# Block 1 retention: rotary partners by GpSimd multiplications in place of TensorE permutation products

## What is computed

```python
def rotary(x, pos):
    half = HEAD_DIM // 2                     # 32
    inv = 1.0 / (ROPE_BASE ** jnp.linspace(0.0, 1.0, half, dtype=jnp.float32))
    ang = pos[:, None] * inv[None, :]
    cos = jnp.cos(ang)[None, :, None, :]
    sin = jnp.sin(ang)[None, :, None, :]
    x1, x2 = x[..., :half], x[..., half:]
    return jnp.concatenate([x1 * cos - x2 * sin, x2 * cos + x1 * sin], axis=-1)

q = rotary(q.reshape(b, s, RET_HEADS, HEAD_DIM), pos)
k = rotary(k.reshape(b, s, RET_HEADS, HEAD_DIM), pos) * (HEAD_DIM ** -0.5)
```

## Time and profile before

| what | value |
|---|---|
| median of three executions | 3490.95 us |
| the profiled execution | 3486.4 us |
| its span, first to last instruction | 3484.6 us |
| mean granted TensorE clock | 0.988 |
| TensorE busy | 3376.5 us, 97% |
| VectorE busy | 1652.7 us, 47% |
| ScalarE busy | 1226.2 us, 35% |
| GpSimd busy | 199.2 us, 6% |

### The profile page before, as it was taken

The page is one execution under the profiler, slowest core; times in us unless marked ns, Lnnn a source line. Parts: engine busy times, 40 slices in busy tenths (PEclk is TensorE's granted clock), DMA queues, the critical chain, the costliest instruction groups (busy, mean ns, idle before and its releaser), DMA issues.

```text
span 3484.6 us, 42143 instructions
## 1 busy us (share of the span) xinstructions
PE 3376.5 (97%) x15726; PEld 2641.3 (76%) x15726; DVE 1652.7 (47%) x2158; ACT 1226.2 (35%) x1831; POOL 199.2 (6%) x247
## 2 busy tenths in 40 slices
PE   8989999999899999999998999999999999999998
PEld 6657888775688877888775688887888776678887
DVE  6755443566444335443545554434443543654433
ACT  4343122432422234222444442234222444542233
POOL 1200000011010000000002310000000001310000
PEclk9999999999999999999999999999999999999999
DMA  6213322221243222332320143333332321033331
GB/s 167 66 43 84 97 97 96 85 79 49 61 106 99 95 92 79 96 98 96 78 64 24 30 104 96 96 97 87 96 97 100 85 73 32 16 89 96 96 96 67
DMA packets 434262, 288.19 MB, mean 83 GB/s; under 512 B 44528, under 2 KB 412316, under 8 KB 433896
## 3 DMA queue, kind: packets, MB, share of 16 engines
q1 hardware_dynamic: 431272, 280.02, 27.7%
q0 software_dynamic: 2736, 4.58, 0.9%
q10 hardware_dynamic: 144, 2.10, 0.2%
HBM read 284.53 MB, written 2.13 MB: 82 GB/s over the span
## 4 chain that ended last, share of the span: by engine, by line
PE 92%; DVE 3%; ACT 3%; issue 2%; DMA 0%; SPq 0%; DVEq 0%; ACTq 0%
PE bank L1964 27%; PE bank L1966 27%; PE bank L1965 27%; PE bank L1974 2%; PE bank L2061 1%; PE bank L2107 1%; PE bank L2083 1%; PE bank L2184 1%; PE bank L2151 1%; PE bank L2448 1%; PE bank L2450 1%; PE bank L2013 1%; PE bank L2035 0%; ACT whi L927 0%; DVE G L1506 0%
## 5 line engine op out<-in xcount | busy, mean ns | idle before, releaser
L1964 PE MATMUL bank<-hh,whi 128*128 128x512 f32 x2832 | 1140.6, 403 | 36.7 <-DVE hl L1418 22.8
L1966 PE MATMUL bank<-hh,wlo 128*128 128x512 f32 x2832 | 1107.9, 391 | 0.0
L1965 PE MATMUL bank<-hl,whi 128*128 128x512 f32 x2832 | 1107.5, 391 | 0.0
L1368 DVE TENSOR_TENSOR wlo<-raw,whi 128x1024 fp32r<-128x1024 f32 (+2 forms) x534 | 642.5, 1205 | 300.6 <-ACT whi L927 285.8
L1964 PEld LDWEIGHTS bank<-hh,whi 128*128 128x128 f32 x2832 | 535.4, 189 | 184.2 <-issue 49.4
L927 ACT ACTIVATE whi<-raw 128x1024 fp32r<-128x1024 f32 (+2 forms) x534 | 546.2, 1034 | 255.2 <-PE bank L1966 254.8
L1965 PEld LDWEIGHTS bank<-hl,whi 128*128 128x128 f32 x2832 | 535.3, 189 | 121.3 <-issue 14.2
L1966 PEld LDWEIGHTS bank<-hh,wlo 128*128 128x128 f32 x2832 | 534.5, 189 | 113.1
L1964 PE MATMUL bank<-fshi,whi 128*128 128x512 f32 (+1 forms) x1358 | 526.6, 388 | 3.5 <-DVE G L1643 2.0
L1966 PE MATMUL bank<-fshi,wlo 128*128 128x512 f32 (+1 forms) x1358 | 523.2, 385 | 0.0
L1965 PE MATMUL bank<-fslo,whi 128*128 128x512 f32 (+1 forms) x1358 | 522.8, 385 | 0.0
(11 more groups left out here) (244 smaller groups left out, 2391.6 us busy)
## 6 DMA issues: line engine op xcount, KB each, us to landing
raw<-in_ffn_w_gate SPq DMA_DIRECT2D x88, 512.0 KB, 3.8
raw<-in_ffn_w_up SPq DMA_DIRECT2D x88, 512.0 KB, 3.8
raw<-in_ffn_w_down SPq DMA_DIRECT2D x88, 512.0 KB, 3.4
raw<-in_w_in SPq DMA_DIRECT2D x78, 512.0 KB, 3.9
raw<-in_w_up SPq DMA_DIRECT2D x64, 512.0 KB, 4.0
raw<-in_w_down SPq DMA_DIRECT2D x64, 512.0 KB, 3.4
raw<-in_w_out SPq DMA_DIRECT2D x16, 512.0 KB, 4.0
raw<-in_w_in SPq DMA_DIRECT2D x18, 256.0 KB, 3.6
```

The source lines that it names most:

```text
L1368: dve.tensor_tensor(slot3(wlo, s, m), slot3(raw, s, m), slot3(whi, s, m).bitcast(F32), ALU.subtract).then_inc(c.lo_done.sem, 1)
L1964: pe.matmul(o, wh, ah, start=start, stop=False)
L1965: pe.matmul(o, wh, al, start=False, stop=False)
L1966: return pe.matmul(o, wl, ah, start=False, stop=stop)
```

## The change

In block 1 the six swap groups of a layer are gone, and with them the permutation matrix. Each is replaced by two steps.

`("spin", name, nth, at)` runs on GpSimd: four tensor_tensor multiplications of 32x512. Each takes 32 rows of the evacuated tile times 32 rows of the sine table, and writes them 32 partitions further up or down into a spare tile. (The signs in the table are turned round accordingly.) The spare tiles alternate: a new one, `half_turn`, and the room of the first gate. Each multiplication waits by semaphore for the one before it. GpSimd's loop of scalings becomes a walk through the list, where spins and scalings alternate as the list has them, and a scaling waits for the last spin before it.

`("spun", nth, at)` runs on VectorE: the tile times the cosines, then plus the spare tile.

The steps are placed anew. Pair t now has eight list entries: rq, spin, rk, spin, rvf, spun, rv, spun. Before it had rq, rk, sq, rvf, sk, rv. The first score product of a pair waits for the second spun, and the first gate's evacuation for all six.

```diff
     def ret_qkv(t):
-        for m, at in (("q", A_RQ), ("k", A_RK)):
-            groups[f"s{m}{t}"] = dict(name=f"s{m}{t}", kind="swap", of=f"r{m}{t}", tile=at + S * t, rows=(0, P), perm="r", tab=3072, frees="dve")
-        return [add(f"rq{t}", "fm", 1664 + 128 * t, frees="act", dst=A_RQ + S * t),
-                add(f"rk{t}", "fm", 2048 + 128 * t, frees="act", dst=A_RK + S * t), ("g", f"sq{t}"),
-                add_turned(f"rv{t}", 2432 + 128 * t, t, 4, dst=A_RV), ("g", f"sk{t}")]
+        return [add(f"rq{t}", "fm", 1664 + 128 * t, frees="act", dst=A_RQ + S * t), ("spin", f"rq{t}", 2 * t, A_RQ + S * t),
+                add(f"rk{t}", "fm", 2048 + 128 * t, frees="act", dst=A_RK + S * t), ("spin", f"rk{t}", 2 * t + 1, A_RK + S * t),
+                add_turned(f"rv{t}", 2432 + 128 * t, t, 4, dst=A_RV), ("spun", 2 * t, A_RQ + S * t), ("g", f"rv{t}"), ("spun", 2 * t + 1, A_RK + S * t)]
...
-    steps += weave(in_order(r0, "rv0"), attend(3, 6), taps(5, 11))
+    steps += weave(r0, attend(3, 6), taps(5, 11))
     steps += weave(in_order(qkv(2), "v2"), attend(6, 8), taps(11, 16))
-    steps += weave(in_order(ret_qkv(1), "rv1"), heads(0), attend(8, 11), taps(16, 23))
-    steps += weave(in_order(ret_qkv(2), "rv2"), heads(1), attend(11, n_att + PV_LAG), taps(23, TAPS))
+    steps += weave(ret_qkv(1), heads(0), attend(8, 11), taps(16, 23))
+    steps += weave(ret_qkv(2), heads(1), attend(11, n_att + PV_LAG), taps(23, TAPS))
...
+                def spin(done_pairs, name, nth, at):
+                    made = b1["groups"][name]
+                    if nth == 0:
+                        pool.wait_ge(decay_in, 16)
+                    if nth >= 2:
+                        pool.wait_ge(c.r_spun.sem, c.r_spun.at(l, nth - 1))
+                    pool.wait_ge(c.evac(made).sem, c.emptied(l, made))
+                    pool.wait_ge(c.scaled.sem, c.scaled.at(l, done_pairs))
+                    for r in range(0, P, 32):
+                        to = r ^ 32
+                        pool.wait_ge(c.r_spin.sem, c.r_spin.at(l, 4 * nth + r // 32))
+                        pool.tensor_tensor(spin_tile(nth)[to:to + 32, :], g(at, S, (r, r + 32)), tab[r:r + 32, 3584:4096], ALU.mult).then_inc(c.r_spin.sem, 1)
+                spun = weighed_pairs = 0
+                for s in b1["steps"]:
+                    if s[0] == "weigh" and s[1] >= EXP_LAG:
+                        if spun:
+                            pool.wait_ge(c.r_spin.sem, c.r_spin.at(l, 4 * spun))
+                        weighed(s[1] - EXP_LAG)
+                        weighed_pairs = s[1] - EXP_LAG + 1
+                    elif s[0] == "spin":
+                        spin(2 * weighed_pairs, *s[1:])
+                        spun += 1
...
+            def spun(c, l, nth, at):
+                if nth == 0:
+                    dve.wait_ge(decay_in, 16)
+                dve.wait_ge(c.r_spin.sem, c.r_spin.at(l, 4 * nth + 4))
+                dve.tensor_tensor(g(at), g(at), tab[:, 3072:3584], ALU.mult).then_inc(c.dve_step.next(), 1)
+                dve.wait_ge(c.dve_step.sem, c.dve_step.now(l))
+                dve.tensor_tensor(g(at), g(at), spin_tile(nth), ALU.add).then_inc(c.r_spun.sem, 1)
...
                     if jt == 0:
-                        need(c, b, l, f"sq{h // 2}", f"sk{h // 2}", f"rv{h // 2}")
+                        need(c, b, l, f"rv{h // 2}")
+                        pe.wait_ge(c.r_spun.sem, c.r_spun.at(l, h // 2 * 2 + 2))
```

More of the change, by code:

```diff
@@ L53 @@
 MLA_SCALE, HEAD_SCALE = float(96) ** -0.5, 0.125
-C_IDENT, C_ONES, C_BLK, C_TRI, C_NONES, C_PERM_R, C_PERM_N, C_VALID = [128 * i for i in range(8)]
-C_WORDS = 7 * 128 + 4
+C_IDENT, C_ONES, C_BLK, C_TRI, C_NONES, C_PERM_N, C_VALID = [128 * i for i in range(7)]
+C_WORDS = 6 * 128 + 4
 SCR_SQ, SCR_RSTD, SCR_TMP, SCR_SQ2 = 0, 1024, 1536, 2560
@@ L85 @@
 SB_AT = [0, 512, 896, 1152]
-ACT_STEPS, DVE_STEPS = (2, 18), (95, 37)
+ACT_STEPS, DVE_STEPS = (2, 18), (89, 37)
 NSA_PAIRS, T_LAG, O_LAG, P_BUFS = 3, 4, 5, 4
@@ L114, in constants @@
     in_head = p % HD
-    partner_r = p - in_head + (in_head + 32) % HD
     partner_n = np.where(in_head < 8, p + 8, np.where(in_head < 16, p - 8, p))
-    for at, partner in ((C_PERM_R, partner_r), (C_PERM_N, partner_n)):
-        c[partner, at + p] = 1.0
+    c[partner_n, C_PERM_N + p] = 1.0
     c[:, C_VALID:C_VALID + QT] = (p[:, None] + P * np.arange(QT)[None, :]) >= 31
@@ L138, in constants @@
     t1[:, 3072:3584] = np.cos(ang)
-    t1[:, 3584:4096] = np.where(in_head < 32, -1, 1)[:, None] * np.sin(ang)
+    t1[:, 3584:4096] = np.where(in_head < 32, 1, -1)[:, None] * np.sin(ang)
     t2 = np.zeros((P, 2048), f)
@@ L479, in build @@
         eps = sb("eps", [P, 1])
+        half_turn = sb("half_turn", [P, S])
         bank = ctx.enter_context(nc.psum_tensor("bank", [P, 8, S], F32))
@@ L577, in counts_of @@
             c.rn_sq = signal("rn_sq", 32, 27)
+            c.r_spin = signal("r_spin", 8 * (HEADS1 // 2), 0)
+            c.r_spun = signal("r_spun", HEADS1, 0)
             c.rn_acc = signal("rn_acc", 10, 7)
@@ L683, in stick_step, with spin_tile @@
             return s // QT, QT - 1 - s % QT, 2 + 2 * (s % 2)
+        def spin_tile(nth):
+            return half_turn[:, :] if nth % 2 else g(MIX + 5 * S)
         def score_banks(e):
@@ L861, in _, with weighed @@
                 tables(1)
-                for j in range(n1):
+                def weighed(j):
                     st = stat[:, j % 4, :]
@@ L1063, in group @@
                 elif kind in ("fm", "uq"):
+                    if gr["name"] == "rg0":
+                        act.wait_ge(c.r_spun.sem, c.r_spun.at(l, HEADS1))
                     if gr["name"] == "rq1":
@@ L1560, in _ @@
             tap_at = [0, 0]
+            def spun(c, l, nth, at):
[5 more added lines that the diff above has]
+                dve.tensor_tensor(g(at), g(at), spin_tile(nth), ALU.add).then_inc(c.r_spun.sem, 1)
             def swap(c, l, gr, bk, evac):
-                if gr["name"] == "sq0":
-                    dve.wait_ge(decay_in, 16)
                 r = gr["rows"]
@@ L1775, in _ @@
                         weigh(c, l, s[1])
+                    elif s[0] == "spun":
+                        spun(c, l, *s[1:])
                     elif s[0] == "taps":
@@ L2149, in group @@
                     need(c, b, l, gr["of"])
-                    at = {"r": C_PERM_R, "n": C_PERM_N}[gr["perm"]]
+                    at = C_PERM_N
                     ins = pe.matmul(bk[0:r[1], :], cs(at, r, r[1]), g(gr["tile"], S, r), start=True, stop=True)
```

## The result

The changed kernel takes 3520.4 us (median), the kernel before beside it 3488.8: a ratio of 1.0084 (95% interval 1.0071 to 1.0097). That is 0.8% slower, and above the predicted range of 3486 to 3509 us.

A forecast was written before the change was run, and what follows sets the result against it. TensorE was taken as the bound, busy 97%. Losses of 1.7 + 1.3 + 0.1 = 3.1 us a layer, 6.2 for both, gave 3492.6 from the profiled 3486.4; with the median 4.6 higher, forecast 3497, range 3486 to 3509.

The forecast's parts named there:

- The spin's price: GpSimd's four 32x512 multiplications for one tile: 6.5 us, bounds 3.2 and 8.5 or a little over.
- The slower rival: GpSimd's queue paces the first stage hard, from a spin of 7.6 us: 3505 at 8.5, 3511 at 9.5; chance 0.27.
- the disturbance: GpSimd and VectorE disturb each other: 0.7 us a tile added to GpSimd's spin.
- scaling 2: GpSimd's attention scaling behind the first spin: 2.46 us long, from 95.5 to 98.0 us, TensorE waiting 1.6 us for it.
- scaling 3: GpSimd's attention scaling behind the second spin: 3.10 us long, ending at 107.7 us, when TensorE's waiting transposes start.
- The stage of pair 0: First head pair of a layer: scalings behind two spins come late, +1.7 us, both products' savings gone.
- the stage of pair 2: Last head pair of a layer: VectorE's queue ends with the second cosine step, +0.1 us, two products' savings lost.
- The port rule: VectorE instructions with two SBUF inputs and GpSimd instructions reading SBUF shut each other out; cited as speaking against the change.
- Nothing stands in a gap: On TensorE, the next instruction follows each removed product at once; 5.9 us a layer removed.
- the most it can bring: Twelve permutation products taken off TensorE in both layers: at most 11.8 us, 0.34% of the run.
- rs8: Score product in head pair 1's stage, waiting for VectorE's last cosine step whatever GpSimd does: +1.3 us a layer.
- rs16: Score product ending head pair 2's stage, waiting for VectorE's addition: 200.1 us by the stage's count, 203.1 in the changed trace.

The follow-up runs named there:

- ceiling run: Against the kernel before: no permutation products, no partners made, GpSimd has its scalings alone, VectorE multiplies by cosines and adds a table; 3480.6 us, ratio 0.9979.
- memset: Changed kernel with GpSimd's four products a tile replaced by memsets that read nothing, partners left out of queries and keys; 3502.4 us, ratio 1.0043.
- one128: Changed kernel with one GpSimd product of 128 rows in place of four of 32, so the rotation is wrong; 3495.6 us, ratio 1.0022.
- memset_filler: Changed kernel with GpSimd's products replaced by memsets and overwritten products put on TensorE ahead of two waits; 3498.7 us, ratio 1.0031.
- free: The ceiling run: kernel before without permutation products and with nobody making partners; 3480.6 us, ratio 0.9979.
- act_late: Kernel before without block 1's permutation products; ScalarE copies the partners, behind the high part of the next weights; 3480.3 us, ratio 0.9980.

## Why the prediction was wrong

**The spin's price was right.** 4 x 1.45 + 0.7 = 6.5 us stood in the sum; 5.3 to 6.2 was measured in layer 0. 32 rows have no discount, and the piece costs 1.35 to 1.41. The 1.12 us that I had estimated from the Trainium skill ("GPSIMD Engine Reference", section 3.1) was less than measured. The slower rival (a spin over 7.6 us) never came about; the time went its way, and further, by other mechanisms.

**The step that failed first: the disturbance was put on GpSimd alone.** I added 0.7 us a tile to the spin, and left VectorE's queue at its undisturbed durations, though the prediction itself calls the effect mutual. Taps in the groups of VectorE from 70 to 220 us, before and after (busy us, mean ns):

```profile
L1552 DVE SCALAR_TENSOR_TENSOR G<-G,prm 128x512 f32<-128x512 f32 x60 | 42.0, 744 | 0.0
```

```profile
L1579 DVE SCALAR_TENSOR_TENSOR G<-G,prm 128x512 f32<-128x512 f32 x60 | 50.9, 888 | 0.0
```

That is 8.9 us in layer 0; the 15 low parts, 20.1 us against 15 x 1.22 = 18.3, add 1.8. The conv taps were not "beside" the change, they were its victims: scaling 2 stretched to 3.83 where the sum has 2.46, the reciprocal for scaling 3 not before 106.24, scaling 3 1.33 us late by it, transposes at 110.58 where the prediction (107.7, and 0.4 for the later start) has 108.1. The stage of pair 0 lost 6.5 us where the sum has 1.7. In the stage of pair 2, where I had +0.1, late evacuations made rk2 wait 2.71 us and the transposes of step 11 2.50. Without reads the run is 18 us shorter. The port rule that I cited from the Trainium skill ("SBUF — State Buffer", section "SBUF: two separate sides") names VectorE's side of the lock as well as GpSimd's; the traces agree (2.69 and 3.11 us beside spins that read, 1.41 beside memsets), and I used half of it.

**The second: a wait was charged at its own length.** The waits were followed by work at 1.2 GHz, and covering four of them gave back 15 us. The ten waits of both layers last 29 us together, so the half clock cost about half as much again. The Trainium skill ("TensorE: Matmul & The Clock Gate", section "Part 1: The HAM clock gate") says that the half clock is the default and that activity lifts it; the windows at 0.51 behind the wait and at 1.00 behind the same wait covered agree. My prediction noted a clock of 1.00 and didn't ask what the change would do to it. The savings of reads and clock (18 and 15) can't be added: with both out it is 22, since a wait that isn't there needs no cover.

**The third: the value of the products.** "Nothing stands in a gap" is true of the trace and was the wrong question. The transposes at 105.97 in the earlier trace rows start 0.14 us after scaling 3 ends (102.40 + 3.43 = 105.83): the products filled a time that a chain through ScalarE, VectorE and GpSimd sets anyway. The formula had this (the first stage takes its two products as lost from a spin of 5.6 us on), but for the whole I called 11.8 us the most it can bring. In the ceiling run 8.5 us had been won at the norms, and 5.5 were left in the median, since the clock fell behind the norms' wait. So 3.3 us of the 11.8 became waits like the 1.09 one, and 3 (by the median) to 4.4 (by the stretches) went by the clock. This step is the smallest of the three: the sum's stages gave the savings away already, and only the ceiling stood too high.

**What held.** rs8: I had VectorE's queue behind the transposes of pair 8, no matter what GpSimd does, and +1.3 us for the stage. Its wait is 4.71 us in after, in memset and in one128 alike, and the stage lost 1.6 by rs8 in all three. Scaling 2's start (95.5, and 0.4 for the start) came at 95.23. And with reads and half clock out, layer 0 lost 3.0 us where the queue sum has 1.5; nearly all of the difference is in the stage of pair 0. The model of queues was sound to that measure; the two things outside of it, stretched operations and half clock, made 22 of the 32 us. For rs16 I had an addition of VectorE as the last wait, at 203.1: in after it waits for nothing, since TensorE itself comes 13.5 us later than that (216.98, less 0.4 for the start); in memset, memset_filler and one128 it waits 1.3 us for that addition. The term of this stage was written +0.1, and my own count (194.1 + 5.96 against 200.11) gives 0.0; this is nothing against the miss.

**Open.** Why the clock falls behind the 2.15 us wait of the norms in some kernels and not in others, and in one layer and not in the other. The last 3.3 us of after's loss in layer 0 are of this kind, and so are the 2.9 and 1.5 us that free loses there; I know no way to forecast them from the trace of before. Whether act_late escapes it by the place of its copies or by luck isn't shown. And what GpSimd's spins would give with another list than the two tried isn't known; in neither of the two are they covered.

## What to carry to other kernels

Before moving elementwise work to GpSimd, list what VectorE does at that time: here its operations with two SBUF inputs stretched while GpSimd read, those with one did not, and the delay landed on whoever waited behind them. ScalarE had room for the same four copies with no such effect, once they stood behind the step that others wait for. A removed product is worth its time only if nothing else ends at the moment when its successor starts: look for the engine whose result landed just then. And a new wait on TensorE costs what it lasts and, in this kernel, half as much again in half-clocked work behind it; a few overwritten products in the wait show how much of a loss is clock. Before a total is read as a gain or a loss of the change, split it where the clock fell: the ceiling run looked 3 us smaller than its queues were.

## What was unexpected of the hardware

- A GpSimd product of 32x512 float32 takes 1.35 to 1.41 us and one of 128x512 1.28: rows are free, pieces are not.
- Waiting for its own semaphore between two such pieces costs GpSimd nothing that can be seen (5.70 us a spin with and without).
- Two VectorE operations of 0.68 and 0.69 us took 1.74 and 1.63 beside four GpSimd products; one with an input from PSUM kept its 1.22 beside four others.
- ScalarE is held for 2.5 us by issuing four transfers of 64 KB, as long as by making the copies itself.
- Behind waits of 2.5 to 4.7 us of TensorE the granted clock was at the 1.2 GHz level in layer 0; behind one of 2.49 in layer 1 it wasn't, and behind one of 2.15 it was in some kernels and wasn't in others.
